# A two-layer float32 decoder trunk: one set of sums moved past the middle of each MLP, a few partial sums left in PSUM, and the squares of one norm added later

## The reference, cut to what matters

```
hn = rms_norm(h, mlp_norm[i])
h = h + jnp.square(jax.nn.relu(hn @ w_mlp_in[i])) @ w_mlp_out[i]      # 1024 -> 4096 -> 1024
hn = rms_norm(h, ple_norm[i])
h = h + (p[i] @ w_ple_up[i]) * jax.nn.sigmoid(hn @ w_ple_gate[i])     # the "embedding"
```

## Time and profile before

| | |
|---|---|
| median of 3 runs | 2432.41 us (2431.59 to 2433.84) |
| the profiled execution's own time | 2426.45 us |
| span in its profile | 2424.7 us |
| mean granted TensorE clock | 0.977 |
| busy: PE / DVE / ACT / POOL | 94% / 69% / 38% / 45% |

### The profile page before, as it was taken

The page is one execution under the profiler, slowest core; times in us unless marked ns, Lnnn a source line. Parts: engine busy times, 40 slices in busy tenths (PEclk is TensorE's granted clock), DMA queues, the critical chain, the costliest instruction groups (busy, mean ns, idle before and its releaser), DMA issues.

```text
span 2424.7 us, 31481 instructions
## 1 busy us (share of the span) xinstructions
PE 2288.2 (94%) x12286; PEld 1845.0 (76%) x12286; DVE 1681.8 (69%) x1967; ACT 923.7 (38%) x1438; POOL 1087.3 (45%) x684
## 2 busy tenths in 40 slices
PE   8998976999999989999998999998999989999997
PEld 6887855787788868888786776676788868888786
DVE  6869178569787887569717355568877796678815
ACT  4120146435333344334313145655333343344315
POOL 4433122135555555556332244564555545566421
PEclk9998988999999999999999999999999999999998
DMA  7382342212443644533113111021435375335111
GB/s 212 99 124 70 108 136 74 88 52 72 154 156 135 225 178 157 191 121 123 53 44 110 38 27 61 19 87 35 157 135 186 142 249 174 123 138 174 44 43 70
DMA packets 226086, 277.87 MB, mean 115 GB/s; under 512 B 33573, under 2 KB 172041, under 8 KB 221833
## 3 DMA queue, kind: packets, MB, share of 16 engines
q1 hardware_dynamic: 212392, 257.14, 32.1%
q10 hardware_dynamic: 13552, 18.81, 3.1%
HBM read 190.53 MB, written 84.21 MB: 113 GB/s over the span
## 4 chain that ended last, share of the span: by engine, by line
PE 76%; DVE 16%; issue 3%; ACT 2%; DMA 1%; ACTq 1%; POOL 0%; DVEq 0%; SPq 0%; POOLq 0%
PE ps L1205 42%; PE ps L828 15%; PE ps L1371 3%; PE ps L979 2%; PE ps L1403 2%; PE ps L1331 1%; DVE hg_queries_keys L2288 1%; PE ps L1344 1%; PE ps L1355 1%; DVE stage L1950 1%; PE ps L1000 1%; PE ps L1015 1%; DVE st_lo L2453 1%; PE ps L895 1%; DVE quads L2473 1%
## 5 line engine op out<-in xcount | busy, mean ns | idle before, releaser
L1205 PE MATMUL ps<-op,st_hi 128*128 128x512 f32 x3584 | 1113.7, 392 | 34.3 <-DVE st_lo L2453 24.1
L1205 PEld LDWEIGHTS ps<-op,st_hi 128*128 128x128 f32 x3584 | 674.9, 189 | 185.1 <-DVE st_lo L2453 29.5
L1205 PE MATMUL ps<-op,st_lo 128*128 128x512 f32 x1792 | 700.5, 391 | 0.0
L672 POOL TENSOR_TENSOR st_lo<-st_raw,st_hi 128x512 fp32r<-128x512 f32 x192 | 312.1, 1626 | 497.1 <-ACT st_hi L1454 495.2
L1205 PEld LDWEIGHTS ps<-op,st_lo 128*128 128x128 f32 x1792 | 338.2, 189 | 71.2
L633 POOL CAST w_hi<-w_raw 128x1024 fp32r<-128x1024 f32 x66 | 73.5, 1114 | 485.9 <-issue 250.0
L1454 ACT ACTIVATE st_hi<-st_sum 128x512 fp32r<-128x512 f32 x256 | 159.9, 628 | 311.4 <-POOL st_sum L664 124.3
L1454 ACT ACTIVATE st_hi<-st_raw 128x512 fp32r<-128x512 f32 x192 | 120.9, 630 | 360.2 <-PE ps L1205 175.8
L2453 DVE TENSOR_TENSOR st_lo<-st_sum,st_hi 128x512 fp32r<-128x512 f32 x256 | 236.8, 931 | 7.4 <-ACT st_hi L1454 6.1
L2517 DVE TENSOR_TENSOR residual<-residual,ps 128x512 f32<-128x512 f32 x192 | 130.4, 681 | 122.6 <-PE ps L1205 122.1
L2533 DVE TENSOR_TENSOR op<-op_raw,op 128x1024 fp32r<-128x1024 f32 x112 | 176.2, 1574 | 16.6 <-ACT op L1454 16.6
(11 more groups left out here) (341 smaller groups left out, 3473.6 us busy)
## 6 DMA issues: line engine op xcount, KB each, us to landing
op_raw<-mid_dram SPq DMA_DIRECT2D x56, 1024.0 KB, 7.5
st_raw<-w_mlp_in_in SPq DMA_DIRECT2D x32, 1024.0 KB, 5.6
mid_dram<-quads SPq DMA_DIRECT2D x32, 1024.0 KB, 3.9
st_raw<-w_mlp_out_in SPq DMA_DIRECT2D x32, 1024.0 KB, 5.4
mid_dram<-mid_sums SPq DMA_DIRECT2D x32, 512.0 KB, 3.5
w_raw<-w_in_even_in SPq DMA_DIRECT2D x20, 512.0 KB, 4.6
residual_dram<-residual ACTq DMA_DIRECT2D x2, 4096.0 KB, 12.4
mid_dram<-mid_last_sum SPq DMA_DIRECT2D x32, 256.0 KB, 2.4
```

Of the source, the lines that this page charges most:

```text
L672: pool.tensor_tensor(SL[r][:, :, :], x, SH[r][:, :, :].bitcast(F32), sub).then_inc(S["st_lo_pool"], 1)
L1205: ins = pe.matmul(PS[:, o, :], w[:, j, :], OP[s][:, x, j, :], start=(fresh and j == 0 and w is SH[r] and x == 0), stop=(j == 3 and w is SL ...
```

## The change

Four parts.

1. **The quads of the last up set (jobs 14 and 15).** `post(t)` places `scaled`, `squared`, the mid sums and the stores. For sets 0 to 6 their slots stay. For set 7 they move by `TURN` = 9 slots, from 111 to 118 to 120 to 127, on DVE, ACT and SP.
2. **First products kept in PSUM.** For down jobs with q = 0 or 1 (`resident`), the product `s` = 0 goes to the fourth bank of its parity (4 or 5) and PE accumulates all four chunks there. Product 3 of these jobs then starts its bank afresh, and chunk 3 adds the resident sum to a fourth quarter of `H` too. The adds L2503 to L2505, the copies of jobs 20 and 21 and the adds L2510 for q = 0 and 1 go.
3. **The opening.** PE runs K quarters 0, 1, 2 of slots 0, 1 and 2, then quarter 3 of each. `sum_squares` moves from behind slot 3 to behind slot 4. On ACT `high(3)` and `high(4)` move ahead of tile 7's operands and tile 7's square behind `x_late(5)`; the four scalings of `x_late(4)` go, since `late_difference` now makes them itself in four 512-column instructions. On DVE `add_squares` is taken off the last tiles' chain, `weight_low(2)` to `(4)` come earlier, and `late_difference` and the first half of `late_last` come ahead of the read of the squares.
4. **The embedding.** ACT writes the squares of the new residual into `GATE[:, m]`, whose gate has just been used, and DVE adds all of them after the last low part. The memset of the sum goes.

`third_sum` changes its sign for up jobs, to go with the turned sign of `late_difference`.

```diff
+TURN = 9
+def resident(g, s):
+    return s == 0 and g >= UP and (g - UP) % 4 < 2
+def post(t):
+    last = UP * SLOTS - 1
+    return divmod(t + 1 if t < last else t + 1 - TURN if t >= last + TURN else 0, 2 * SLOTS)
...
 # PE
-                    elif s == 0:
+                    elif resident(g, s):
+                        if g < UP + 2:
+                            pe.wait_ge(S["st_ev"], ev(i, g - 2, 3))
+                    elif s == 0 or s == 3 and resident(g, 0):
...
+                for steps in ((0, 1, 2), (3,)):
+                    for n in range(3):
+                        product(n, steps)
+                for n in range(3, PRODUCTS):
+                    product(n, range(4))
+                    if n == 4:
                         sum_squares(norm)
...
 # ACT
-                x_operands(i, norm, 7)
                 high(3)
                 high(4)
+                x_operands(i, norm, 7)
+                x_late(i, 5)
+                x_square(norm, 7)
                 high(5)
                 high(6)
-                x_late(i, 4, 0)
+                x_late(i, 6)
                 high(7)
-                x_late(i, 5, 1)
-                x_late(i, 6, 1)
+                copy(0, 0)
                 cast_late(i, 4, 9, 9)
-                copy(0, 0)
                 copy(1, 0)
...
 # DVE, after a down job
-                    if s == 0 and c == 0:
-                        tt(h12, h12, PS[:, a_, :], add)
-                        tt(h22, h22, PS[:, a_, :], add)
-                        tt(h21, h21, PS[:, a_, :], add).then_inc(S["st_ev"], 1)
-                        return
+                    if c == 3 and s == 4 and resident(g, 0):
+                        dve.wait_ge(S["st_ev"], ev(i, g, 3))
+                        own(tt(h11, h11, z, add))
...
 # DVE, opening
+                weight_low(3)
                 x_lows(KT - 1)
-                weight_low(3)
+                weight_low(4)
+                add_squares(norm, KT - 2)
+                add_squares(norm, KT - 1)
                 end_norm()
-                weight_low(4)
                 weight_low(5)
+                late_difference()
+                late_first()
                 dve.wait_ge(S["ss_done"], norm + 1)
                 dve.tensor_scalar(RSTD[:, :], flat(PS[:, 4:6, :]), 1.0 / D, EPS, ALU.mult, ALU.add).then_inc(S["ss_read"], 1)
-                late_difference()
-                late_last()
...
 # DVE, the loop over t
-                    if k < SETS // 2 and r == 13:
-                        scaled(g)
-                    if 1 <= k <= SETS // 2:
-                        if r == 0:
-                            scaled(g - 1)
...
+                    kp, rp = post(t)
+                    if 1 <= kp <= SETS // 2:
+                        first, second = 2 * kp - 2, 2 * kp - 1
+                        if rp == 0:
+                            scaled(first)
+                        if rp == 1:
+                            scaled(second)
...
 # DVE, embedding
-                start_norm()
...
-                low(after, KT - 1, ROW[gain[0]] + gain[1])
+                x_low(KT - 1)
+                dve.nop().then_inc(S["sq_used"], 1)
+                for m in range(1, KT):
+                    dve.wait_ge(S["sq_done"], 8 * after + m + 1)
+                    dve.wait_ge(S["sq_used"], 8 * after + m + CREDIT)
+                    tt(SUMSQ[:, :], GATE[:, 0, :] if m == 1 else SUMSQ[:, :], GATE[:, m, :], ALU.add).then_inc(S["sq_used"], 1)
```

More of the change, by code:

```diff
@@ L1193, in operand, with product @@
                         pe.wait_ge(S["op_ready"], n + X_READY + 14 * ((g - UP) // 4) + 2 * s + j // 2 + 1)
-                for n in range(PRODUCTS):
+                def product(n, steps):
                     g, s = product_at(n)
                     a_, b_, c_, d_ = BANKS[g % 2]
[L1198 to L1202, removed]
+                    r = n % RINGS
+                    o = (d_ if resident(g, s) else a_, b_, c_, d_ if g < UP else a_, b_, c_, b_)[s]
+                    fresh = g < UP + 2 if resident(g, s) else s < 3 or s == 3 and (g < UP or resident(g, 0))
+                    if 0 in steps:
+                        weights(g, s)
+                        bank(g, s)
+                    for j in steps:
                         operand(g, s, j)
@@ L1462, in settle @@
                 act.nop().then_inc(S["passed"], 1)
[L1464 to L1468, removed]
-                    fn(XAh[:, bass.ds(m, 1), :].rearrange("p a t -> p (a t)"), hm, ACT.Identity,
-                       scale=COLS[:, bass.ds(m + (ROW[gain] + g0), 1)]).then_inc(S["x_hi_done"], 1)
-                    wait("sq_used", m + 8 * norm + CREDIT)
-                    fn(SQ[:, :], hm, ACT.Square).then_inc(S["sq_done"], 1)
             def root(n):
@@ L1810, in mlp @@
                 cast_late(i, 6, 10, 11)
-                high(10)
-                high(11)
-                high(12)
-                high(13)
+                for n in range(10, 14):
+                    high(n)
                 for t in range(10, PRODUCTS + 1):
@@ L2511, in evict_down @@
                         return
-                    if (g, 0) not in COPIES and c == 0:
-                        dve.wait_ge(S["st_ev"], ev(i, g, 0))
                     if s in (4, 5):
@@ L2551, in mlp @@
                 for m in range(1, KT):
-                    if i and m == KT - 1:
+                    if m == KT - 1:
                         weight_low(2)
@@ L2600, in mlp @@
                         evict_up(g - 1, 6)
-                    if t > UP * SLOTS and product_at(t - 1) not in COPIES:
+                    if t > UP * SLOTS and product_at(t - 1) in EVICTIONS:
                         evict_down(*product_at(t - 1))
@@ L2635, in mlp, with embed @@
                 end_norm()
-            def embed(i, norm, nroot, after, gain):
+            def embed(i, norm, nroot, after):
                 u0 = UNIT[f"gate{i}"]
@@ L2660, in embed @@
                     if m:
-                        low(after, m - 1, ROW[gain[0]] + gain[1])
-                low(after, KT - 1, ROW[gain[0]] + gain[1])
+                        x_low(m - 1)
+                x_low(KT - 1)
[4 more added lines that the diff above has]
+                    tt(SUMSQ[:, :], GATE[:, 0, :] if m == 1 else SUMSQ[:, :], GATE[:, m, :], ALU.add).then_inc(S["sq_used"], 1)
+                dve.wait_ge(S["sq_used"], 8 * after + KT + CREDIT)
                 end_norm()
```

130 lines of the change are left out of this document (73 added, 57 removed).

## The result

The changed kernel takes 2408.4 us, the median of four runs (2407.84 to 2408.79), against 2432.28 us for the kernel before on the same chip: a ratio of 0.9901, interval 0.9884 to 0.9918. The forecast was 2392, with a low end of 2384 and a high end of 2406: the time lies above it.

The account below looks back on a forecast made before the run. The prediction took DVE to be what PE waits for. Gains of 25.6 (middle), 6.7 (opening) and 8.2 us (embedding), 40.5 in all, gave 2385.95 us profiled and a median of 2392, range 2384 to 2406.

Parts of the forecast that it names:

- What bounds the kernel: Whole kernel: PE is busy 94% of the span, and the engine named in its waits is DVE each time.
- Part 1 and the three adds: Slots 112 to 120: 18.0 us of work leaves DVE's full stretch, the stall goes, gain 13.2 + 12.4 = 25.6 us.
- what was to stay at slot 113: Wait for POOL's low part behind an 8.52 us weight load: 0.4 us in MLP 0, 0.7 in MLP 1.
- Slot 120 alone takes 5.0, slot 121 3.1, so DVE is 2.7 us late and level again in slot 122: Slots 120 to 126: DVE's 18.2 us of work fits in 19.0, with 8.2 us of slack; no cost taken.
- The shared interface: Rival, 0.08: the twelve moved instructions meet POOL's sums at 1 us each, costing 3 us a layer: 2398 us.
- The gain is by how much DVE's stream gets shorter: Opening, to slot 22: DVE's stretch falls to 44.3 and 44.1 us, gaining 2.7 and 4.0, together 6.7 us.
- The bounds, 0 to 11.4: Opening's gain: 11.4 us with all idle time gone, 0 if ACT or POOL holds DVE up by as much.
- The rival that the opening gives nothing back: Rival, 0.16: DVE wins on L2565 what it loses on ACT's squares, so 6.7 us less gain: 2399 us.
- The new wait at slot 6: Opening: slot 6's product needs L2565; 1 us in hand in MLP 0, 2 us late in MLP 1, hidden until slot 22.
- Part 4: Embedding: six adds of squares and the memset go, 8.2 us gained, 3.6 us a tile, four us of cover.
- The sum: 25.6 + 6.7 + 8.2 = 40.5 us off the profiled 2426.45; the median, 5.96 above, comes to 2392 us.
- three signs of being wrong: A new wait in slots 121 to 131, DVE's opening stretch not 3 to 4 us shorter, or PE waiting at L859.

## Why the prediction was wrong

- **What bounds the kernel** was right: in the changed kernel every stall that moved ended on DVE, and the stretches without an edit differ by no more than they do among kernels that share their code.
- **Part 1 and the three adds**: 25.6 us forecast, 25.6 measured in slots 112 to 120. Of what was to stay at slot 113, MLP 1 keeps a wait of 0.6 us and MLP 0 none. Right in size. Apart, the parts gave 21.6 and 5.9 us.
- **"Slot 120 alone takes 5.0, slot 121 3.1, so DVE is 2.7 us late and level again in slot 122"**: this step failed, for 6.7 us. It put all work at undisturbed durations, and took DVE to be on time at slot 120. In the profile after DVE is already behind there, by refills that POOL stretches from 1.2 to 1.7 to 2.3 us, and the moved work is stretched as well. The shared interface was a rival with 0.08, priced at 3 us a layer from the twelve moved instructions alone, at 12 us more work. It came: 3.2 and 3.4 us. With POOL's sums out, 2.7 and 2.9 of these go. That the price fits is luck: from 870 to 912 us the twelve moved instructions take 14.6 us for 10.2, only 4.4 more, and the eight refill halves another 4.3 and the eight weight tiles 3.1, which the rival did not count. The Trainium skill (Advanced Engine Details and Errata, GPSIMD Details) says that GpSimd shares a read and a write interface with VectorE, in conflict with VectorE instructions that have two SBUF inputs. The trace agrees: L2553, with two, takes 1.75 us for 1.2, and L2534, with one input in PSUM, stays at 0.675. A wait of 1.3 us that the sum did not have either, the second job's last sum behind the first one's store, stands in the same slots; what it costs alone was not tried.
- **"The gain is by how much DVE's stream gets shorter"**: this step failed, for 12.1 us, the most of the miss: 6.7 us to be gained, 5.4 lost. Two terms of it. The stream was counted at 42.3 and 41.3 us busy and was 44.3 in both. What the sum left out is that the late difference, cut in four and moved, meets POOL: L2457 takes 4.8 us for 2.6 in both layers, two of its four instructions 1.77 us for 0.74. About half of that goes with POOL's sums. (The 3.27 us of L2465 are no part of the miss: L2443 had them before, and they are in the 42.67.) The sum had cited a 3.27 us instruction as a warning and then priced this new neighbour without it. And ACT's queue was not followed past the square. The cast for product 6 holds up highs, loads and at last the root, for which DVE waits 2.5 us; with the cast behind the highs, 1.9 of these go in MLP 0. In MLP 1, where the wait is 2.6 us, it needs the read of the squares moved as well: there slot 6's wait makes the same highs late. Against the sum the stretches ended 2.4 and 3.0 us late, and behind them stand another 2.4 and 4.2 us, 12.0 together; of the 4.2, 2.6 are the wait for the root, and the rest is about what the clock lost behind slot 22's stall, 6 us at 0.72 of it in the window below, where before it stayed at 1.00.

```profile
1706.00:1712.00 6.00, 5.85 (x19) 0.72 0.46 134
```

  The bounds, 0 to 11.4, left out any loss. The rival that the opening gives nothing back looked at ACT too, but at its squares, and stopped at zero.
- **The new wait at slot 6** was named, "2 us late" in MLP 1, none in MLP 0; it is 5.4 and 3.1. That it is hidden until slot 22 was right for the order as it stands: with it gone in MLP 0 and down to 2.2 us in MLP 1, neither opening got shorter. It was not right for MLP 1 once the cast is behind, where the second edit gave 2.6 us.
- **Part 4**: 8.2 forecast, 9.0 measured, 3.6 us a tile, adds covered by 3.0 us for 4.2. Right.
- **The sum**: with part 3 at +5.4, the middle at -19.0 and part 4 at -9.0, it is -22.6 for -40.5; the medians differ by 23.9. Of the three signs of being wrong two came: slots 121 to 131 have new waits, and DVE's opening stretch is 0.3 and 1.0 us shorter, not 3 to 4. PE does not wait at L874.

Open is what decides whether a stall of some 2.5 us brings the clock down. The same stall cost 3 us more in one execution than in another. The Trainium skill (TensorE: Matmul & The Clock Gate, Part 1: The HAM clock gate) says that the window of the monitor that gates the clock is free-running and is not reset by the start of a kernel. The runs here fit that and do not test it. Open too are the price of part 4 alone in medians, and what POOL's low parts cost beside L2457.

## What to carry to other kernels

A price from an undisturbed instruction holds only where its neighbours on the other engines stay. Before work is moved on VectorE, list what GpSimd does in the stretch it goes to, price instructions with two SBUF inputs there at their stretched duration (1.4 to 1.9 times here for the long ones), and count from how late the engine arrives, not from the slot's start. When a reorder shortens one engine's stream, follow each other engine's queue to the same end: a cast that moved 7 us later held up weight loads and a square root 20 us on. And let an unknown effect of a reorder reach below zero in the range.

## What the runs showed of the hardware

- VectorE and GpSimd stretch each other; the first is shown by leaving GpSimd's sums out, the second only by what stands beside it. L2553 alone takes 1.21 us and beside GpSimd 1.72 to 2.32; GpSimd's L687 takes 1.28 us at its shortest in the opening, 1.74 at its longest there, and some 2.0 beside VectorE's refills (two in 4.00 us).
- The price of a stall on PE is not fixed. Waits of 2.6 us ran on at a granted clock of 1.00 in one execution and at 0.51 for 6 us in another. An opening with 2.9 us less waiting (5.6 us for 8.5 from slot 0 to 22 of MLP 0) took as long. A single profile with a stall in it is uncertain by that much for each, and only medians or several profiles can tell a change of 2 us.
